# Head sums of the third attention on all 128 rows and columns, the second group behind two spreads

## What is computed

```python
h = rms_norm(x, norm1_pre[i])
proj = h @ w_in[i]
q, k, v, z, xbc, dt_raw, gates = split_cols(proj, IN_SPLITS)
q = rms_norm(q.reshape(b, s, N_KV_HEADS, Q_PER_KV, HEAD_DIM), q_norm[i])
k = rms_norm(k.reshape(b, s, N_KV_HEADS, HEAD_DIM), k_norm[i])
q, k = axial_rope(q, ang_row, ang_col), axial_rope(k, ang_row, ang_col)
attn_out = gqa_attention(q, k, v) @ w_attn_proj[i]
ssd_y = ssd_branch(z, xbc, dt_raw, ...)   # per head: exp(cumsum_l - cumsum_s), masked, both directions
```

## Time and profile before

| | us |
|---|---|
| median of 3 runs (lowest, highest) | 2258.36 (2256.61, 2261.64) |
| profiled execution, time | 2258.43 |
| its span, first to last instruction | 2256.6 |
| PE busy | 2156.5 |
| DVE, ACT, POOL busy | 1175.3, 1004.7, 945.6 |

### The profile page before, as it was taken

One profiled execution on the slowest core, in us unless ns is written; L12 is line 12 of the kernel. 1 busy time (PEld: TensorE's weight loads), 2 busy tenths in 40 slices (PEclk: granted clock), 3 DMA queues, 4 the chain that ended last, 5 costly groups with the idle time before them and its releaser, 6 DMA issues.

```text
span 2256.6 us, 27665 instructions
## 1 busy us (share of the span) xinstructions
PE 2156.5 (96%) x10564; PEld 1768.2 (78%) x10578; DVE 1175.3 (52%) x1857; ACT 1004.7 (45%) x2027; POOL 945.6 (42%) x714
## 2 busy tenths in 40 slices
PE   8999899999999898899999999999999999999997
PEld 6788778888877677778888877777678887888886
DVE  3445565554335678565554355776854326444323
ACT  6666444444225566244443244756543335322222
POOL 4555563344446664553433442322313343222233
PEclk9999999999999999899999998999999999999999
DMA  4111122322222321123222211111012222232231
GB/s 165 55 57 57 57 94 96 106 98 95 97 89 80 95 66 60 57 77 106 98 94 103 88 62 68 57 38 38 20 66 94 98 99 75 94 103 103 87 103 54
DMA packets 29842, 183.03 MB, mean 81 GB/s; under 512 B 3984, under 2 KB 4112, under 8 KB 11920
## 3 DMA queue, kind: packets, MB, share of 16 engines
q1 hardware_dynamic: 29712, 181.27, 23.5%
HBM read 174.97 MB, written 2.10 MB: 78 GB/s over the span
## 4 chain that ended last, share of the span: by engine, by line
PE 83%; DVE 8%; ACT 4%; issue 3%; POOL 1%; DMA 1%; SPq 0%; POOLq 0%; DVEq 0%; ACTq 0%
PE PS L1511 81%; PE PS L1641 1%; DVE bQS L2249 1%; PE PS L1748 1%; DVE XL L2326 0%; POOL LO L2805 0%; DMA RAW<-wall 0%; DVE aQS L2249 0%; ACT HI L1834 0%; ACT bP L2052 0%; DVE bP L2553 0%; DVE T_f L2321 0%; DVE YH L2351 0%; ACT bQS L2030 0%; PE PS L1689 0%
## 5 line engine op out<-in xcount | busy, mean ns | idle before, releaser
L2805 POOL TENSOR_TENSOR LO<-RAW,HI 128x512 fp32r<-128x512 f32 (+2 forms) x382 | 541.8, 1434 | 605.2 <-ACT HI L1834 605.2
L1511 PE MATMUL PS<-XH,HI 128*128 128x512 f32 (+1 forms) x1584 | 632.1, 399 | 7.7 <-POOL LO L2805 2.1
L1511 PE MATMUL PS<-XH,LO 128*128 128x512 f32 (+1 forms) x1584 | 620.8, 392 | 0.0
L1511 PE MATMUL PS<-XL,HI 128*128 128x512 f32 (+1 forms) x1584 | 617.0, 394 | 3.6 <-DVE XL L2326 1.7
L1834 ACT ACTIVATE HI<-RAW 128x512 fp32r<-128x512 f32 (+3 forms) x668 | 366.0, 607 | 171.7 <-PE PS L1511 168.3
L2249 DVE TENSOR_TENSOR LO<-RAW,HI 128x512 fp32r<-128x512 f32 (+2 forms) x286 | 304.9, 1070 | 246.0 <-ACT HI L1834 245.5
L1511 PEld LDWEIGHTS PS<-XH,HI 128*128 128x128 f32 (+1 forms) x1584 | 299.6, 189 | 72.3 <-issue 7.5
L1511 PEld LDWEIGHTS PS<-XL,HI 128*128 128x128 f32 (+1 forms) x1584 | 297.2, 189 | 71.5 <-DVE XL L2326 8.7
L1511 PEld LDWEIGHTS PS<-XH,LO 128*128 128x128 f32 (+1 forms) x1584 | 298.6, 188 | 64.3
L1511 PE MATMUL PS<-HH,HI 128*128 128x512 f32 x528 | 205.4, 389 | 0.0
L1511 PE MATMUL PS<-HL,HI 128*128 128x512 f32 x528 | 205.4, 389 | 0.0
(11 more groups left out here) (412 smaller groups left out, 3298.6 us busy)
## 6 DMA issues: line engine op xcount, KB each, us to landing
RAW<-wall SPq DMA_DIRECT2D x138, 1024.0 KB, 4.9
RAW<-wall SPq DMA_DIRECT2D x24, 896.0 KB, 4.6
bROT<-bTQ SPq DMA_DIRECT2D x64, 64.0 KB, 2.0
RAW<-wall SPq DMA_DIRECT2D x5, 512.0 KB, 3.3
XF<-xT SPq DMA_DIRECT2D x4, 512.0 KB, 5.5
outT<-XR SPq DMA_DIRECT2D x8, 256.0 KB, 2.0
FP<-cfp SPq DMA_DIRECT2D x1, 1024.0 KB, 6.9
MKF<-cmask SPq DMA_DIRECT2D x1, 704.0 KB, 10.9
```

Source lines behind the costliest of these rows:

```text
L1511: return e.matmul(out, a, b, start=start, stop=stop)
L2805: return e.tensor_tensor(out, x, h.bitcast(F32), ALU.subtract)
```

## The change

HSUM gets 128 columns and HSPR 128 rows for each of three tiles, with zeros where nothing stood; both move into the buffer XS, and the factors HRS have 128 rows. So `cp1` and `cp2` are matmuls of 128 rows by 128 columns of weights, and root and reciprocal run on 128 rows. HSUM and HSPR are built in a new step `hc`, put right after `rps` of `c0`; `half` keeps only the scalars. `squares(1)` waits until `cp2` of ROPED[1] (tile 4) is in the list: `cp1 1` is put one tick behind `cp2 4` and `cp2 1`. RF gets 128 rows, of which ACT zeroes rows 64 to 127 in the step `rf`, and `sh` reads 128 rows of SEL and RF.

```diff
@@ second(), deviation()
         freed[6] = ("rps", put("rps", n))
+        if n == "c0":
+            put("hc")
...
         def squares(g):
-            while not all(squared[n] for n in GROUPS[g]):
+            while not all(squared[n] for n in GROUPS[g]) or (g and ("cp2", ROPED[1]) not in steps):
                 yield
...
-    HSUM = TN[:, 48:72]
-    HRS = [by4(XS[:, :])[0:8, :, 128 * g:128 * g + 128] for g in range(2)]
-    HSPR = by4(XS[:, :])[0:8, 0:3, 256:384]
+    HRS = [by4(XS[:, :])[:, :, 128 * g:128 * g + 128] for g in range(2)]
+    HSPR, HSUM = (by4(XS[:, :])[:, 0:3, 128 * g:128 * g + 128] for g in (2, 3))
...
-    RF = sb("cRF", 512, F32R, R0 + 117 * K, 64)
+    RF = sb("cRF", 512, F32R, R0 + 117 * K)
@@ tensor
-                    m = mm(PS[bank][0:8, :], HSUM[:, 8 * j:8 * j + 8], SQ5[n], j == 0, j == len(group) - 1)
+                    m = mm(PS[bank][:, :], HSUM[:, j, :], SQ5[n], j == 0, j == len(group) - 1)
...
-                    mm(PS[b][:, :], SEL[0:64, d:d + 1].to_broadcast([64, 128]), RF[:, :], True, False)
+                    mm(PS[b][:, :], SEL[:, d:d + 1].to_broadcast([128, 128]), RF[:, :], True, False)
@@ scalar
-                act(HRS[a[0]], by4(PS[bank][0:8, :]), ACT.Sqrt, bias=EPS6[0:8, :]).then_inc(SEM["cst1"], 1)
+                act(HRS[a[0]], by4(PS[bank][:, :]), ACT.Sqrt, bias=EPS6).then_inc(SEM["cst1"], 1)
...
                 e.wait_ge(*when("srf", *step))
+                act(RF[64:128, :], NEGC[64:128, 8:9].to_broadcast([64, 512]), ACT.Copy)
                 act(RF[0:32, :], PS[bank][0:32, :], ACT.Copy).then_inc(SEM["srfa"], 1)
@@ vector
             elif kind == "half":
+                c = sm["sw0"][0]
+                e.tensor_scalar(SM[:, c:c + 72], SM[:, c:c + 72], 0.5, None, ALU.mult).then_inc(SEM["cconst"], 1)
+            elif kind == "hc":
                 e.memset(HSUM, 0.0).then_inc(s_vv, 1)
                 vv += 1
                 e.wait_ge(s_vv, vv)
                 for j in range(3):
-                    e.tensor_copy(HSUM[:, 10 * j:10 * j + 2], BLK[:, 0:65:64])
-                c = sm["sw0"][0]
-                e.tensor_scalar(SM[:, c:c + 72], SM[:, c:c + 72], 0.5, None, ALU.mult).then_inc(SEM["half"], 1)
+                    e.tensor_copy(HSUM[:, j, 2 * j:2 * j + 2], BLK[:, 0:65:64])
+                e.tensor_copy(HSPR.rearrange("p j (i n) -> p j i n", i=2),
+                              IDN[:, 0:6].rearrange("p (j i o) -> p j i o", i=2, o=1).to_broadcast([128, 3, 2, 64])).then_inc(SEM["cconst"], 1)
...
             elif kind == "cp1":
-                if a[0] == 0:
-                    e.tensor_copy(HSPR.rearrange("p j (i n) -> p j i n", i=2),
-                                  IDN[0:8, 0:6].rearrange("p (j i o) -> p j i o", i=2, o=1).to_broadcast([8, 3, 2, 64]))
```

More of the change, by code:

```diff
@@ L203 @@
     "dol": (("ol", 1),),
-    "half": (("half", 1),),
+    "half": (("cconst", 1),),
+    "hc": (("cconst", 1),),
     "cqe": (("csq", 1), ("cqe", 1)),
@@ L1718, in tensor @@
             elif kind == "cp1":
-                e.wait_ge(*when("half", "half"))
+                e.wait_ge(*when("cconst", "hc"))
                 group = GROUPS[a[0]]
@@ L2159, in scalar @@
                 if j == CONV[0]:
-                    e.wait_ge(*when("half", "half"))
+                    e.wait_ge(*when("cconst", "half"))
                 if j2 is not None:
```

## The result

| | before | after |
|---|---|---|
| median of 17 runs (lowest, highest), us | 2256.76 (2252.59, 2263.62) | 2249.13 (2244.91, 2255.76) |
| profiled execution, its span, us | 2258.43, 2256.6 | 2252.04, 2250.2 |
| mean granted clock | 0.983 | 0.983 |

The ratio is 0.9970, 95% interval 0.9961 to 0.9979: 6.8 us less, between 4.7 and 8.8. The forecast was 2250.2 in 2246 to 2257, and "faster" (more than 4.5 us) was the likeliest sign; both hold. Of the two parts the scan brought what I gave it and the stage half of it, as the trace shows.

The account below looks back on a forecast made before the run. PE was taken as the bound (83% of the chain), at half clock for 20.5 us around the head norms. Half 0.35, stage 4.4 and scan 3.5 summed to 8.2 us less: 2250.2 us, range 2246 to 2257.

Parts of the forecast that it names:

- What bounds the kernel, and why the clock fell: Around the head norms: PE bounds the chain; matmuls leaving rows empty, not idle time, suspected for 20.5 us at half clock.
- rival 4: Zeros do not count, or first bare wait drops the clock until cx: 2263.3 us (0.06), 2259.8 with scan's gain (0.05).
- My own sign for it: At the first gap: if the clock is 1.0 in cp2 4, the slower rival is out.
- half: Early step losing the memset and three copies: PE sooner by 0.35 us, between 0 and 1.1.
- hc: New DVE step between rps and cqe 0, some 2.2 us: cost 0, or 1 us if its cover went.
- The stage, walked at full clock: From cp1 0 to cx 4: 6.5 us sooner, 7.8 with the 1.3 us from cx 4's start.
- The two gaps: PE idle before cp2 0 and before cp2 2, waiting for root and reciprocal: 2.2 and 2.1 us.
- The clock in the walk: One short fall behind each gap, half of 3.4 us each: minus 3.4, so the stage gives 4.4 us (0 to 7.8).
- The scan: sh with 128 rows: 0.5 us a head, 4.0 us over eight heads, later ones up to 1.5; taken as 3.5 (0 to 6).
- rival 3: In the scan, the gaps around the 64-row weights stay: 2253.7 us, chance 0.10.
- some would be caught: In the scan: some of the gain caught by ACT and DVE, so 3.5 us taken.
- The sum: Whole kernel: 0.35 + 4.4 + 3.5 = 8.2 us less, so 2250.2 us.

Follow-up runs that it names:

- cp2_8rows: rows_only with cp2 reading 8 rows of HSPR and HRS again; one time, 2252.05 us.
- cp2_64rows: rows_only with cp2 on 64 of the 128 rows of HSPR and HRS; one time, 2253.13 us.
- rows_only: Kernel before plus the change's full-size cp1, cp2 and hc, with cp1 1 in its old place and the old scan; median 2253.2 us, ratio 0.9981.
- fill: Changed kernel plus two 512-column fp32 matmuls, results overwritten, before cp2 0 and before cp2 2; median 2245.46 us, ratio 0.9953 to the kernel before.
- rows_order: Changed kernel without the scan's part, SEL and RF on 64 rows again; median 2252.74 us, ratio 0.9983 to the kernel before.
- no_order: Changed kernel without the wait of squares(1), cp1 1 right behind cp1 0 again; median 2244.15 us, ratio 0.9947 to the kernel before.
- cp1_8cols: rows_only with cp1 on 8 columns of HSUM, root and reciprocal on 8 rows; one time, 2250.45 us.

## Why the prediction was right or wrong, point by point

- **What bounds the kernel, and why the clock fell.** Right, and now shown: `cp2_8rows` and `cp2_64rows` differ from `rows_only` in the rows of `cp2` alone, and the kernels around them agree. The first half of rival 4, that zeros don't count, is out in every kernel with full rows. My own sign for it failed, though: I wanted the clock at 1.0 in `cp2 4`, and `cp2 4` and `cp2 1` ran at 0.50 (from 1381.61, in the piece from 1378.9 to 1385.7). The second half of rival 4, a fall at about 1379 from the first bare wait, is what came; it is out only because the clock was back before `cx 4`.
- **`half`.** 0.35 forecast, 0.17 found, and 0.09 more ahead of `cp1 0`. **`hc`** cost nothing: the fifth `cqe` still waits 3.06 us for PE.
- **The stage, walked at full clock.** 7.8 us forecast with the clock up. `fill` is that case by experiment: 36.99 to 29.66, 7.3 us. The two gaps were put at 2.2 and 2.1 us, found at 2.29 and 2.29; root and reciprocal on 128 rows, left at 0.68 and 3.28, came out at 0.69 and 3.35.
- **The clock in the walk.** This is the term that was mis-sized. I took one fall of 3.4 us behind each gap, minus 3.4. It was 10.2 us at 0.50, minus 5.1: the first fall was 6.8 us long. The stage gave 2.2 us, not 4.4: 7.3 - 5.1. The row I sized it by the earlier trace rows shows one fall of 3.4 us, and one row doesn't say how long the next lasts. `rows_order` had 13.7, so even the length in the same stage isn't fixed.
- **The scan.** 3.5 us forecast; in the profile 4.49 in 12 heads less 0.94 in the rest, 3.55. The place was right (RF to mask 0.23 to 0.24 us; rival 3 is out); that the lost time is a drain of the engine, as I read it, no row shows. That some would be caught was right too: PE's wait for DVE's `cYT` grew from 1.68 to 2.90 us, and a fall of 3.4 us at 1624.7 follows, which I hadn't in the sum. All seven kernels with the full-height scan have a fall of 3.4 or 6.8 us there, of the seven others only rows_only and cp2_64rows. The split was off: the eight heads that I gave 4.0 us brought 3.3 (51.20 less 47.88), and the next three, which were to bring nothing of their own, brought 1.3 before PE had to wait (up to 1630 there are four heads, not five). By the times of runs it is 2.9, with 7.7 in the comparison named above. The rule of the Trainium skill that stood against it, "TensorE: Matmul & The Clock Gate", part 3 (a load overlaps only where row groups differ), did not decide here: in the stretch from 1558.60 the loads of full-height weights are busy 39.04 of 51.20 us while PE is busy 50.34.
- **The sum.** 8.2 forecast, 6.4 found in the profile, 6.8 by the ratio. Without 1.7 us of luck in the first layers the profile would show 4.7: of the forecast's terms 6.0 came (0.25, 2.2, 3.55), and 0.90 before the scan and 0.46 behind it, for which I had no term, were lost again. The time fits in part because the median of the kernel before came out 1.6 us lower over 17 runs than over the three that I had.
- **What I didn't ask.** The new place of `cp1 1` was taken as part of one package. Against `no_order` it costs 5.2 us: each of my own numbers for it (gaps of 2.2 and 2.1 us and their falls) stood in my walk, and the wait before the first scores, the only thing on the other side, I never priced for the old place with the clock up.

Open: why rows_only had 10.2 us at 0.50 in the tail of the scan and cp1_8cols, with the same scan, none.

## What to carry to other kernels

An engine that is busy all the time can still run at half clock: look at the granted clock beside the busy share, and at how many rows the matmuls around the fall fill. Padding the small fp32 matmuls to full height with zeros took no PE time that the traces show. It was worth 9.5 us at the place, and 4.3 to 9.0 by the times of runs, depending on what else was changed. Half height held the clock too, but going to a lower height and back cost 0.36 us around a single matmul. When a packaged change brings a gain, undo its parts one by one: here one of the three cost 5.2 us, and a matmul whose product nobody reads, put into a bare wait, was worth 3.8, or 5.1 at the place.

## What the runs showed of the hardware that I had not expected

- 8-row fp32 matmuls between 160-column ones: 17.10 us at 0.50 with PE busy 17.10 of 17.10 (cp2_8rows); at 64 rows, none.
- Around one fp32 matmul of 512 columns among full-height ones, 8 rows cost 0.36 us more than 128 (1.44 against 1.08) and 64 rows the same 0.35 to 0.36 (cp2_8rows, cp2_64rows, rows_only).
- The falls behind the same two gaps were 6.8 and 3.4 us (twice) and 6.8 and 6.8 (rows_order); a wait of 3.73 to 3.77 us was followed by a fall of 6.8 us in rows_only, of 3.4 in cp1_8cols and by none in no_order.
- The reciprocal of 512 columns takes 3.28 us on 8 rows and 3.35 on 128: rows are nearly free on DVE, as root's 0.68 and 0.69 show for ACT.
